# Expert weights in whole tiles: four ring places, four lead places used twice, and a reordered router

## The reference

```
logits = t @ w_router                                  # 256 x 8
top_vals, top_idx = top_k(logits, 2)
gates = softmax(top_vals)
combine = sum(one_hot(top_idx, 8) * gates)
for e in range(8):                                     # D_FF_EXPERT = 3584
    he = (silu(t @ w_gate[e]) * (t @ w_up[e])) @ w_down[e]
    out = out + combine[:, e:e+1] * he
return rmsnorm(h + out, final_norm)
```

## Time and profile before

| | us |
|---|---|
| median of three runs | 2178.97 |
| lowest, highest | 2176.01, 2182.1 |
| the profiled execution, its own time | 2182.77 |
| its span, first to last instruction | 2180.7 |
| mean granted TensorE clock | 0.988 of full speed |

### The profile page before, as it was taken

The page is one execution under the profiler, slowest core; times in us unless marked ns, Lnnn a source line. Parts: engine busy times, 40 slices in busy tenths (PEclk is TensorE's granted clock), DMA queues, the critical chain, the costliest instruction groups (busy, mean ns, idle before and its releaser), DMA issues.

```text
span 2180.7 us, 67375 instructions
## 1 busy us (share of the span) xinstructions
PE 2114.9 (97%) x30418; PEld 1945.7 (89%) x30418; DVE 837.9 (38%) x2085; ACT 465.8 (21%) x1074; POOL 24.7 (1%) x43
## 2 busy tenths in 40 slices
PE   9999999999999999999997899999999999999998
PEld 8889999856999986899986789999999999999997
DVE  4357676314766655467759520101010101010102
ACT  3432112113311134211023221111111111111112
POOL 1000000000000000000000000000000000000000
PEclk9999999999999999999998999999999999999999
DMA  9241444240334423324431338999999999999997
GB/s 394 93 173 72 162 174 175 81 169 8 139 150 169 160 97 136 155 117 174 168 142 40 116 117 327 413 416 410 418 410 418 409 418 409 418 417 416 418 417 287
DMA packets 78407, 534.35 MB, mean 245 GB/s; under 512 B 9106, under 2 KB 9235, under 8 KB 41939
## 3 DMA queue, kind: packets, MB, share of 16 engines
q1 hardware_dynamic: 74450, 519.82, 59.3%
q0 software_dynamic: 3840, 12.85, 1.6%
HBM read 523.00 MB, written 9.63 MB: 244 GB/s over the span
## 4 chain that ended last, share of the span: by engine, by line
PE 65%; DMA 4%; DVE 2%; ACT 1%; issue 1%; DVEq 0%; SPq 0%; ACTq 0%
PE ps L1866 24%; PE ps L1224 12%; PE ps L1882 11%; PE ps L1266 7%; DMA slot<-in_w_moe 4%; PE ps L1141 4%; PE ps L1633 2%; PE ps L1616 1%; DVE scr L2549 0%; PE ps L1813 0%; PE ps L1157 0%; PE ps L1503 0%; PE ps L1489 0%; PE ps L1096 0%; PE ps L1570 0%
## 5 line engine op out<-in xcount | busy, mean ns | idle before, releaser
L1866 PE MATMUL ps<-scr,slot 128*64 128x88 f32 x14336 | 595.4, 241 | 11.1 <-issue 5.4
L1866 PEld LDWEIGHTS ps<-scr,slot 128*64 128x64 f32 x14336 | 562.8, 137 | 22.1 <-issue 12.4
L2698 DVE TENSOR_TENSOR scr<-scr,ps 128x88 f32<-128x88 f32 x224 | 55.1, 246 | 727.1 <-ACT scr L982 727.1
L1882 PE MATMUL ps<-scr,slot 128*64 128x88 f32 x7168 | 315.5, 239 | 1.9 <-issue 1.9
L1882 PEld LDWEIGHTS ps<-scr,slot 128*64 128x64 f32 x7168 | 292.0, 137 | 5.1 <-issue 5.1
L1266 PE MATMUL ps<-scr,slot 128*128 128x256 f32 x1056 | 237.6, 380 | 1.6 <-DVE scr L2369 1.6
L1266 PEld LDWEIGHTS ps<-scr,slot 128*128 128x128 f32 x1056 | 196.6, 191 | 26.0 <-DVE scr L2369 2.0
L982 ACT ACTIVATE scr<-ps 128x88 f32<-128x88 f32 x224 | 54.5, 243 | 743.8 <-PE ps L1866 743.8
L1224 PE MATMUL ps<-vtok,slot 128*128 128x128 f32 x1056 | 139.6, 275 | 0.0
L1224 PEld LDWEIGHTS ps<-vtok,slot 128*128 128x128 f32 x1056 | 128.8, 192 | 0.2
L1224 PE MATMUL ps<-vtok,proj 128*128 128x128 f32 x1056 | 128.7, 275 | 0.0
(11 more groups left out here) (412 smaller groups left out, 2058.4 us busy)
## 6 DMA issues: line engine op xcount, KB each, us to landing
slot<-in_w_moe SPq DMA_DIRECT2D x224, 1024.0 KB, 12.2
slot<-in_w_moe SPq DMA_DIRECT2D x224, 512.0 KB, 12.2
slot<-in_w_ffn SPq DMA_DIRECT2D x33, 3072.0 KB, 10.8
slot<-in_w_even_in SPq DMA_DIRECT2D x3, 3072.0 KB, 27.2
slot<-in_w_odd_qk SPq DMA_DIRECT2D x2, 3072.0 KB, 10.6
slot<-in_w_s_glu SPq DMA_DIRECT2D x2, 3072.0 KB, 11.9
slot<-in_w_odd_v SPq DMA_DIRECT2D x2, 2048.0 KB, 8.4
slot<-in_w_even_in SPq DMA_DIRECT2D x2, 1536.0 KB, 10.6
```

Source lines behind the costliest of these rows:

```text
L1866: m = pe.matmul(gate_up(j, k)[s:s + STRIP], w[:, o:o + STRIP], xg[:, c], start=c == 0, stop=c == KD - 1, skip_group_check=True)
L1882: m = pe.matmul(y_sum(d)[s:s + STRIP], w[:, o:o + STRIP], hid[j][:, 0:CAP], start=False, stop=False, skip_group_check=True)
L2698: dve.tensor_tensor(hid[f % 4][:, 0:CAP], gbuf[f % 4][:, 0:CAP], gate_up(f, 1), ALU.mult).then_inc(hid_ready, 1)
```

## The change

- A place holds a whole tile, 12 KB in each partition, two places to a slot. There are eight: 0 to 3 (lead) and 4 to 7 (ring). A tile comes in one transfer of 128 rows of 12 KB, with one semaphore for each place.
- SP loads tiles 0 to 7 as slots come free. Then the four lead places, each once its down is done, get tiles 220 to 223. Then the ring is refilled with tiles 8 to 219, each place once its down is done.
- PE takes tiles 220 to 223 from the lead places. The last two groups of four tiles are written out for it.
- `hrow`, `xl` and `returned` move to other SBUF tiles; POOL's wait on `moe_free` and DVE's before `hrow` go.
- Router: on PE four filler products stand where the gain-row products stood, and those follow the position counts. On ACT the Exp of the gates comes ahead of the two row copies. `gather(1)` follows the first four tiles. PE's wait on the row copies moves from the head of the experts to its first use.

```diff
 RING = 4
+PLACES = 2 * RING
...
+TILES = EXPERTS * FE_TILES
...
-        lead_slots, ring_slots = ([(len(LOADED) - SLOTS + k) % SLOTS for k in some]
-                                  for some in ((0, 1), (2, 3)))
...
-        hrow = lead[0][:, 0:2 * D].rearrange("p (g d) -> p g d", g=2)
-        xl = lead[0][0:CAP, 2 * D:3 * D]
-        returned = lead[1][:, 0:4 * D].rearrange("p (n d) -> p n d", n=4)
+        tile_slots = [(len(LOADED) - SLOTS + h // 2) % SLOTS for h in range(PLACES)]
+        places = [slots[s][:, h % 2 * (UP + DOWN):(h % 2 + 1) * (UP + DOWN)]
+                  for h, s in enumerate(tile_slots)]
+        ups, downs = [x[:, 0:UP] for x in places], [x[:, UP:UP + DOWN] for x in places]
+        hrow = proj[:, 8:16].rearrange("p a n -> p (a n)").rearrange("p (g d) -> p g d", g=2)
+        xl = proj[0:CAP, 16:20].rearrange("p a n -> p (a n)")
+        returned = [yT[:, 4:8]..., xbp[:]..., rgw[:]..., part(34, 4)]
...
-            last = EXPERTS * FE_TILES // RING - 1
-            sp.wait_ge(up_ready, 2 * (FT0["moe"] + RING) + 2)
-            load_up(0, 2 * RING)
-            with sp.Fori(2, last) as i:
-                for h in range(RING):
-                    sp.wait_ge(up_ready, i * (2 * RING) + (2 * (FT0["moe"] + h - RING) + 4))
-                    load_up((h + 1) % RING, i * RING + (h + 1))
-                    sp.wait_ge(moe_free, i * RING + h + 1)
-                    load_down(h, i * RING + h)
+            def load_tile(h, unit):
+                sp.dma_start(places[h], a["w_moe"][bass.ds(unit, 1), :, :].rearrange(
+                                 "o p n -> p (o n)")).then_inc(moe_loaded[h], 16)
+
+            for h in range(PLACES):
+                sp.wait_ge(slot_free, left(tile_slots[h]))
+                load_tile(h, h)
+            for h in range(RING):
+                sp.wait_ge(moe_free, RING + h + 1)
+                load_tile(h, TILES - RING + h)
+            with sp.Fori(2, TILES // RING - 1) as i:
+                for h in range(RING):
+                    sp.wait_ge(moe_free, i * RING + h + 1)
+                    load_tile(RING + h, i * RING + h)
...
             pool.wait_ge(mo["rows"], 3)
-            pool.wait_ge(moe_free, RING + RING)
...
             def router():                                      # ACT
                 act.activation(stat[:, 0, 0:1], ones[:, 0:1], ACT.Sqrt)
                 take_tokens(1)
+                act.wait_ge(rt["diff"], 2)
+                act.activation(tiny[:, GA:GA + 1, 0:2], tiny[:, GA:GA + 1, 0:2], ACT.Exp
+                               ).then_inc(rt["exp"], 1)
                 for b in range(2):
...
-                act.wait_ge(rt["diff"], 2)
-                act.activation(tiny[:, GA:GA + 1, 0:2], ..., ACT.Exp).then_inc(rt["exp"], 1)
...
             def router():                                      # PE
                 pe.wait_ge(tile_taken, TILE0["s5_glu"] + 2 * KD)
-                for c in range(KD):
-                    m = pe.matmul(ps[:, 6 + c // 4, ...], v("final_norm", c)..., ident, ...)
-                    if c % 4 == 3:
-                        m.then_inc(fin["row"], 1)
+                busy(4, 5)
                 pe.wait_ge(mo["sel"], 2)
...
+                for c in range(KD):
+                    m = pe.matmul(ps[:, 6 + c // 4, ...], v("final_norm", c)..., ident, ...)
+                    if c % 4 == 3:
+                        m.then_inc(fin["row"], 1)
...
-                def up(j, loads, inputs=None):
+                def up(j, place, loads, inputs=None):
+                    pe.wait_ge(moe_loaded[place], loads)
...
-                def four(e, i, last=False, first=False):
+                def four(e, i, first=False, before_last=False, last=False):
...
-                    here = None if first else at(16, 0)
+                    lead = first or last
                     for j in range(RING):
-                        if j < RING - 1:
-                            up(j + 1, here)
+                        here = j if lead else RING + j
+                        if j + 1 < RING:
+                            up(j + 1, here + 1, 16 if first else 32 if last else at(16, 0))
+                        elif before_last:
+                            up(0, 0, 32, at(2, 3))
                         elif not last:
-                            up(0, at(16, 16), at(2, 3))
+                            up(0, RING, at(16, 16), at(2, 3))
                         down(j, here, at(RING, FT0["moe"] + j + 1))
...
                 gather(0)
-                gather(1)
-                up(0, None, 1)
+                up(0, 0, 16, 1)
                 open_sums(None)
                 four(0, 0, first=True)
+                gather(1)
                 with pe.Fori(1, GROUPS) as i:
                     four(0, i)
                 turn_rows(16)
                 open_sums(2)
+                pe.wait_ge(fin["rowtaken"], 2)
                 turn_sums(2)
...
-                with pe.Fori(0, GROUPS - 1) as i:
+                with pe.Fori(0, GROUPS - 2) as i:
                     four(EXPERTS - 1, i)
-                four(EXPERTS - 1, GROUPS - 1, True)
+                four(EXPERTS - 1, GROUPS - 2, before_last=True)
+                four(EXPERTS - 1, GROUPS - 1, last=True)
...
-                pe.wait_ge(fin["rowtaken"], 2)
...
                         if e == 0 and f in (RING, RING + 1):   # DVE
                             g = f - RING
-                            dve.wait_ge(moe_free, RING + RING)
                             dve.tensor_scalar(hrow[:, g], vtok[:, g], col[:, 2 + g:3 + g], None,
```

More of the change, by code:

```diff
@@ L314, in build_program @@
         combined, first_copied = sem("combined"), sem("first_copied")
-        moe_up_loaded = [sem(f"moe_up_loaded{i}") for i in range(RING)]
-        moe_down_loaded = [sem(f"moe_down_loaded{i}") for i in range(RING)]
+        moe_loaded = [sem(f"moe_loaded{i}") for i in range(PLACES)]
         moe_free = sem("moe_free")
@@ L428, in build_program @@
         mix0 = {"even_out": 0, "odd_out": KD, "mla_o": 2 * KD}
-        lead_slots, ring_slots = ([(len(LOADED) - SLOTS + k) % SLOTS for k in some]
-                                  for some in ((0, 1), (2, 3)))
[L433 to L444, removed]
-        hrow = lead[0][:, 0:2 * D].rearrange("p (g d) -> p g d", g=2)
-        xl = lead[0][0:CAP, 2 * D:3 * D]
-        returned = lead[1][:, 0:4 * D].rearrange("p (n d) -> p n d", n=4)
+        tile_slots = [(len(LOADED) - SLOTS + h // 2) % SLOTS for h in range(PLACES)]
[4 more added lines that the diff above has]
+        xl = proj[0:CAP, 16:20].rearrange("p a n -> p (a n)")
+        returned = [yT[:, 4:8].rearrange("p a n -> p (a n)"),
+                    xbp[:].rearrange("p a n -> p (a n)")[:, 0:D],
+                    rgw[:].rearrange("p k j n -> p (k j n)"), part(34, 4)]
         where = part(25)[:, 16:64].rearrange("p (n c) -> p n c", c=8)
@@ L1724, in router @@
                           skip_group_check=True).then_inc(mo["pos"], 1)
[L1726 to L1740, removed]
+                for c in range(KD):
+                    m = pe.matmul(ps[:, 6 + c // 4, c % 4 * P:c % 4 * P + P],
+                                  v("final_norm", c).to_broadcast([P, P]), ident, start=True, stop=True,
+                                  skip_group_check=True)
+                    if c % 4 == 3:
+                        m.then_inc(fin["row"], 1)
             def experts_dense():
@@ L1765, in experts_dense, with expert, place @@
                               skip_group_check=True)
-                def expert(e, first):
-                    def up(f):
-                        w = up_weights(e, f, first)
+                def expert(e, first=False, last=False):
+                    def place(f):
+                        if first and f < RING or last and f >= FE_TILES - RING:
+                            return f % RING
+                        return RING + f % RING
+                    def up(f):
+                        if first and f < RING:
+                            pe.wait_ge(moe_loaded[f], 16)
+                        elif last and f >= FE_TILES - RING:
+                            pe.wait_ge(moe_loaded[f % RING], 32)
+                        else:
+                            pe.wait_ge(moe_loaded[RING + f % RING], e * (16 * GROUPS) + 16 * (f // RING))
+                        w = ups[place(f)]
                         for k in range(2):
@@ L1772, in up @@
                                 o = (k * KD + c) * P
-                                m = pe.matmul(pair(f, k), w[:, o:o + P], hT[:, c], start=c == 0,
-                                              stop=c == KD - 1, skip_group_check=True)
+                                m = pe.matmul(pair(f, k), w[:, o:o + P], hT[:, c],
+                                              start=c == 0, stop=c == KD - 1, skip_group_check=True)
                             m.then_inc(up_ready, 1)
                     def down(f):
-                        w = down_weights(e, f, first)
```

(13 more changed lines are left out.)

39 lines of the change are left out of this document (3 added, 36 removed).

## The result

The changed kernel takes **2273.17 us** (median of 4 runs, 2269.01 to 2275.05) against 2178.21 for the kernel before on the same chip: a ratio of 1.043 (1.041 to 1.045), 4.3% slower. I had forecast 2172, with 2187 as the upper end. The time went the other way, and it lies 86 us above that end.

The account below looks back on a forecast made before the run. The prediction took the experts to be bound by weight transfers. Its terms, 6.2 - 1.0 - 16.5 + 4 = -7.3 us, gave 2172 us from the median of 2179.0, with a range of 2160 to 2187.

Parts of the forecast that it names:

- What bounds the kernel: In the experts, weight transfers at 3.768 us a tile set the pace; PE alone only 0.13 us a tile faster.
- Where the ring's stream starts: Start of the experts: first ring refill waits for the down of tile 4, +6.2 us, bounds 5 and 8.
- The last four tiles: End of the experts: tiles 220 to 223 load early in the idle DMA gap, -1.0 us, bounds 0 and -2.
- Row length: Expert weight stream: 12 KB rows reach 426 GB/s, 3.69 us a tile in place of 3.768, -16.5 us.
- Rival 2: Expert weight stream: no rate gained, 12 KB rows run at 417.5 GB/s; +9 us, 2188; chance 0.20.
- A shallower queue: Ring refills: later issue lets DMA run dry when PE is over 1.1 us late at expert changes, +4 us.
- The closing sentence: Ring: prediction fails if row length doesn't set the rate, or a landing alone takes over 7.2 us.
- Rival 3: Seven expert changes: DMA holes stay open, with code stalls on top, +14 in place of +4, 2182 us; chance 0.20.

Follow-up runs that it names:

- e5: Kernel before with three quarters of each tile's up products left out on PE, so transfers alone set the pace: 2164.94 us, ratio 0.994.
- e2: Changed kernel with two transfers a tile, the up place refilled right after its up as in the kernel before: 2182.17 us, ratio 1.0017.
- e10: Kernel before with only the router edits and the new order of the first gathers: 2177.04 us, ratio 1.0007.
- e6: Changed kernel with three quarters of each tile's up products left out on PE: 2157.86 us, 0.991 of the full kernel before.
- e1: Changed kernel with each tile in two transfers, 8 KB and 4 KB rows, both issued after the down: 2269.24 us, ratio 1.042.
- e9: Changed kernel with a quarter of each tile's up products left out, PE 3.03 us a tile: 2201.18 us, ratio 1.011.
- e7: e2 with the refill of the up place half a tile later: 2181.96 us, ratio 1.0029.
- e11: Changed kernel, but each 12 KB row pairs the up part of tile n+1 with the down part of tile n: 2171.09 us, ratio 0.997.
- e8: Kernel before with PE's loop bodies of the first six experts written out to eight tiles, not four: 2242.92 us, ratio 1.030.

## Why the prediction was wrong, by its own steps

- **What bounds the kernel**: right. Before, the stream of weights; e5 repeats 3.767 without PE in the way.
- **Where the ring's stream starts, +6.2**: near in place, not tested as a price. The first up came 6.7 us after the position sums in place of 9.9, 3.2 earlier (forecast 2.8). The first refill was issued at 1323.7, 32.0 us after the sums in place of 26.6, so 5.5 later. But the stream wasn't last afterwards, and the up of tile 8 came only 0.7 later, counted from the same sums.
- **The last four tiles, -1.0**: right. -1.1 from up 219 on. They came in the gap, 300 GB/s from 1303 to 1318.
- These two terms give +5.2, and e2 measured +4.4. That is no proof of the first: e2 refills an up place ahead of the down, so it has only the 1.2 us of the term by which tile 4 comes later, and e10, which has these alone, measured nothing.
- **Row length, -16.5**: right. 3.69 a tile when nothing else is last (e6). In the changed kernel it did not show: the stream was never last. Rival 2 (no rate gained) falls.
- **A shallower queue, +4 with bounds 0 and 14**: this is the step that failed. At equal rows it is 87 us (e1 against e2); in the sum, where it also swallows the -16.5, it would have had to be 106 (95.0 = 6.2 - 1.0 - 16.5 + 106.3). I had the mechanism in full: a refill issued one PE tile after the landing of g and due three tiles later, 7.4 us on. I compared that with a landing of 6.1 us, interpolated between lone transfers of 4.8 and 10.1 us. It is 8.5. And the reissue comes 4.1 us after a landing, not 3.64, so the refill is due after 7.0 us. The margin was -1.5 us and not +1.1, and it is missed at each tile, not at seven expert changes. The closing sentence, "or if a landing alone takes over 7.2 us, since then PE waits at every tile", is near what came true: the landing alone stays under 7.2, the one in the ring doesn't. I gave it no chance and no price. The same step with 8.5 and 4.1 gives (8.5 + 4.1) / 3 = 4.2, and 212 x (4.20 - 3.69) = 108 us, against the 106.3 that the sum lacks.
- **Rival 3, queue runs dry, +14**: right in kind, but it kept the holes to the seven changes.
- The Trainium skill has in "DMA: Bandwidth & Descriptors", section "Anatomy of one DMA", a fit of 2.0 us plus bytes over 436 GB/s, for another way of issuing. For a tile an estimate by it is 5.6 us, and would have misled in the same direction as my 6.1. The chains of the changed kernel and of e9 show 7.8 to 9.3 with one or two more transfers in the queue.

Why 8.5 and not 6.1 is settled in part, by the changed kernel's own trace. Tiles 6 and 7 were issued 0.4 us apart with no tile ahead of them; the first landed after 6.6 us (so 6.1 was near for a lone tile). Tiles 220 to 223 were issued some 3.6 us apart, also with no tile ahead of them, and landed after 7.7, 7.6, 8.2 and 9.7 us, every one above the 7.0 that the ring leaves:

```profile
L490 SPq DMA_DIRECT2D slot<-in_w_moe x2: 328/380/431, 1286.9 to 1287.3; - x2
...
DMA to landing us min/median/max: 6.6/8.2/9.9
...
L490 SPq DMA_DIRECT2D slot<-in_w_moe x4: 328/328/328, 1305.4 to 1316.3; - x4
...
DMA to landing us min/median/max: 7.6/8.0/9.7
```

So it is the landing of a lone tile that was the wrong figure for a ring whose refills follow each other by a tile. What lengthens it is not shown. The engines don't move the bytes more slowly throughout; they do it with holes between, as windows of the changed kernel show:

```profile
1465.00:1472.00 7.00, 5.99 (x153) 5.67 (x151) 0.49 (x2) 1.65 (x3) 0.00 (x0) 1.00 1.00 421
1488.50:1490.50 2.00, 2.00 (x59) 2.00 (x57) 0.04 (x1) 0.25 (x1) 0.00 (x0) 1.00 0.86 252
```

In a hole single packets of 12 KB last up to 2.4 us, where the median is 460 ns; from 1530 to 1606 the mean is 497 ns, and 465 in e6. Such packets count as busy, and so the share stays at 0.97 while 376 GB/s flow.

## What to carry to other kernels

Where a refill waits for the consumer, write the loop down: (landing + time from landing to reissue) / tiles in that turn, and compare it with the transfer's own pace; below it nothing is lost (e7), above it each tile pays. Take the landing from a stretch in which transfers follow each other as they will in the ring, and where only lone ones exist, let the range hold 1.4 times their figure, which is what it came to in this one case. Before giving up depth for longer rows, look whether the parts of a row can be chosen so that they are used together (e11).

## What was unexpected of the hardware

- A loop body of PE of eight tiles (768 matmul records) costs 65 us over one of four (e8), with stalls of up to 9.4 us and 62 more packets of instructions (151 against 89).
- The share of the DMA engines can't tell a full stream from a starved one: 0.97 at 376 GB/s, 1.02 at 414 to 418. The landing time and GB/s can, GB/s best in windows of a few us.
- The part ahead of the experts, nearly the same code in all, took between 1281.9 and 1291.6 us in the profiled executions, up to the position sums. A single profile's span can be off by some 8 us for this reason. Counted from the position sums to the last down, before takes 879.5, after 968.3, e2 881.4, e10 877.4, e11 868.1.
